# One half of an output projection multiplied inside the softmax branch that precedes it

## The reference

```python
ret = retention(...).reshape(B, S, RET_WIDTH) * silu(rg)        # 512 features
att = nsa(...).reshape(B, S, NSA_WIDTH) * silu(ng)              # 512 features
mixed = concatenate([ret, att], axis=-1)                        # 1024
y = rmsnorm(mixed @ w_out[l], g_post[l])                        # projection 2
x = x + gate * y
# second block
f = swiglu(rms_norm(h, g_ffn1_pre), w_ffn1_gate, w_ffn1_up, w_ffn1_down)
h = h + 0.5 * rms_norm(f, g_ffn1_post)
```

## Time and the profile before

| | us |
|---|---|
| three runs, median (lowest to highest) | 1502.58 (1501.13 to 1503.46) |
| span of the profiled execution | 1500.5 |
| TensorE busy | 1452.3 (97%) |
| VectorE busy | 828.7 (55%) |
| ScalarE busy | 683.7 (46%) |
| GpSimd busy | 201.9 (13%) |
| DMA engines, share of the span | 27.2% for the queue that loads the weights |

### The profile page before, as it was taken

The page is one execution under the profiler, slowest core; times in us unless marked ns, Lnnn a source line. Parts: engine busy times, 40 slices in busy tenths (PEclk is TensorE's granted clock), DMA queues, the critical chain, the costliest instruction groups (busy, mean ns, idle before and its releaser), DMA issues.

```text
span 1500.5 us, 22048 instructions
## 1 busy us (share of the span) xinstructions
PE 1452.3 (97%) x8524; PEld 1226.9 (82%) x8524; DVE 828.7 (55%) x1455; ACT 683.7 (46%) x1302; POOL 201.9 (13%) x319
## 2 busy tenths in 40 slices
PE   7999999899999999999999999989999999999997
PEld 4887876678988888888998777769988888888996
DVE  6678646776645444432275577574754444422474
ACT  4565536676542222221363556676532232321563
POOL 0000000443310000000130222451300000000221
PEclk9999999999999999999999999999999999999999
DMA  9542440004033333333404211503133333332321
GB/s 365 197 167 85 124 157 10 1 2 169 2 99 98 98 98 98 94 95 94 152 3 167 71 57 43 169 16 99 33 109 98 94 92 96 103 105 92 120 85 56
DMA packets 42148, 146.71 MB, mean 98 GB/s; under 512 B 4673, under 2 KB 7121, under 8 KB 41682
## 3 DMA queue, kind: packets, MB, share of 16 engines
q1 hardware_dynamic: 37986, 128.99, 27.2%
q0 software_dynamic: 3072, 15.71, 2.8%
q10 hardware_dynamic: 1008, 0.89, 0.2%
HBM read 141.39 MB, written 4.19 MB: 97 GB/s over the span
## 4 chain that ended last, share of the span: by engine, by line
PE 84%; DVE 9%; ACT 3%; issue 2%; DMA 1%; POOL 0%; DVEq 0%; SPq 0%; ACTq 0%; POOLq 0%
PE B L285 22%; PE B L287 22%; PE B L286 22%; PE CROW_P L285 3%; PE CROW_P L287 3%; PE CROW_P L286 3%; PE B L1789 2%; PE B L2025 1%; DVE AL L1381 1%; DVE WADA L1143 1%; PE CROW_P L1868 1%; ACT T L622 1%; PE CROW_P L1768 1%; ACT AH L622 1%; DVE WL L1110 1%
## 5 line engine op out<-in xcount | busy, mean ns | idle before, releaser
L285 PE MATMUL B<-UH,WH 128*128 128x512 f32 (+1 forms) x1008 | 374.7, 372 | 4.6 <-DVE WL L1110 3.7
L287 PE MATMUL B<-UH,WL 128*128 128x512 f32 (+1 forms) x1008 | 372.3, 369 | 0.0
L286 PE MATMUL B<-UL,WH 128*128 128x512 f32 (+1 forms) x1008 | 372.3, 369 | 0.0
L622 ACT ACTIVATE WH<-RAW 128x1024 fp32r<-128x1024 f32 x174 | 182.6, 1052 | 120.0 <-DMA RAW<-in_stream 111.6
L285 PEld LDWEIGHTS B<-UH,WH 128*128 128x128 f32 x1008 | 190.4, 189 | 38.0 <-issue 5.0
L286 PEld LDWEIGHTS B<-UL,WH 128*128 128x128 f32 x1008 | 190.3, 189 | 32.0
L287 PEld LDWEIGHTS B<-UH,WL 128*128 128x128 f32 x1008 | 190.2, 189 | 32.0
L1110 DVE TENSOR_TENSOR WL<-RAW,WH 128x1024 fp32r<-128x1024 f32 x94 | 116.0, 1240 | 143.8 <-ACT WH L622 143.7
L1462 DVE TENSOR_TENSOR WL<-RAW,WH 128x1024 fp32r<-128x1024 f32 x80 | 98.0, 1226 | 76.7 <-ACT WH L622 73.9
L622 ACT ACTIVATE T<-B 128x256 f32<-128x256 f32 (+5 forms) x186 | 86.5, 465 | 109.9 <-PE B L287 63.3
L622 ACT ACTIVATE T<-T 128x512 f32<-128x512 f32 (+3 forms) x131 | 68.7, 525 | 130.8 <-DVE T L1466 119.2
(11 more groups left out here) (419 smaller groups left out, 3146.2 us busy)
## 6 DMA issues: line engine op xcount, KB each, us to landing
RAW<-in_stream SPq DMA_DIRECT2D x202, 512.0 KB, 3.7
WADA<-in_w_ada SPq DMA_DIRECT2D x8, 1024.0 KB, 16.7
RAW<-in_stream SPq DMA_DIRECT2D x16, 384.0 KB, 3.5
WADA<-in_w_ada SPq DMA_DIRECT2D x2, 2048.0 KB, 11.5
W<-in_w POOLq DMA_DIRECT2D x2, 2048.0 KB, 12.1
X<-in_x SPq DMA_DIRECT2D x2, 1024.0 KB, 11.0
DECAY<-in_decay POOLq DMA_DIRECT2D x1, 2048.0 KB, 9.6
X<-in_x POOLq DMA_DIRECT2D x2, 1024.0 KB, 8.2
```

The lines of the kernel that those rows point to most:

```text
L285: nc.tensor.matmul(out, lh, rh, start=start, stop=False, **kw)
L286: nc.tensor.matmul(out, lh, rl, start=False, stop=False, **kw)
L287: return nc.tensor.matmul(out, ll, rh, start=False, stop=stop, **kw)
L622: return nc.scalar.activation(out, in_, func, **kw)
```

## The change

Retention's half of projection 2 is taken out of it and made of 32 steps. A step is one contraction tile k of 0 to 3 of one chunk c of 0 to 7, in the full width of 512 tokens (`part_step`). One step runs in each of rounds 5 to 9 and 12 to 35 of the softmax branch, after the scores and ahead of the transposes; the last three follow the branch. The steps use bank B5 alone, so the scores' ring has three banks, and scores m wait for `exp` at 2m-1, the first unit of round m-1. ScalarE copies each full chunk out of B5 to SBUF (`part_out`, into PART, 512 columns), after the round's first exponential.

The weights of projection 2 are loaded as pairs of half chunks, retention's halves first, into other places, and they are split earlier: high parts ahead of rounds 4, 9, 14, 19, 27, 34, 35 and 37, low parts ahead of rounds 5, 10, 15, 20, 28, 35 and twice 37. The first step of a chunk waits for the low part. What follows the branch (`mix_out`) multiplies tiles 4 to 7 only; VectorE adds PSUM and PART into Y_H, and ScalarE squares Y_H. The MLP's first four chunks go tile by tile through all four (`first_up`), first t = 0 and then t = 1, and `n_stats(1)` stands after all of them.

```diff
-        KEPT_AT = {"p1": (64, 72, 80, 88), "p2": (16, 24, 64, 72, 80, 32, 40, 88), ...
+        KEPT_AT = {"p1": (64, 72, 80, 88), "p2": ("w0", 16, 24, "w0", 16, 24, 64, 72), ...
+        PART = [at(f"PART{m}", OFF_U + ((16 if m < 4 else 0) + 2 * (m % 4)) * KB, [P, SEQ]) for m in range(8)]
-        S_BANK, PT_BANK = [B[2], B[3], B[4], B[5]], [B[6], B[7]]
+        S_BANK, PT_BANK = {"nsa": [B[2], B[3], B[4]], "band": [B[2], B[3], B[4], B[5]]}, [B[6], B[7]]
+        PART_ROUNDS = [5, 6, 7, 8, 9] + list(range(12, 36))
+        PART_STEPS = [(c, k) for c in range(8) for k in range(4)]
+        PART_AT = {m: PART_STEPS[n] for n, m in enumerate(PART_ROUNDS)}
+        PART_LEFT = PART_STEPS[len(PART_ROUNDS):]
+        PART_ENDS = {m: c for m, (c, k) in PART_AT.items() if k == 3}
# SyncE
+                if D_P2 <= d < D_P2 + 8:
+                    half, pair = divmod(d - D_P2, 4)
+                    sp.dma_start(RAW[:, slot, :].rearrange("p (m c) -> p m c", m=2),
+                                 a["stream"][D_P2 + 2 * pair:D_P2 + 2 * pair + 2, :, 512 * half:512 * half + 512].rearrange("m p c -> p m c")
+                                 ).then_inc(raw_here[slot], 16)
# ScalarE
+            def part_out(c):
+                wait(act, E["part"], c + 1)
+                E["part_out"].mark(f(PART[c][:, :], B[5][:, :], ACT.Copy))
...
                             tag["exp"].mark(f(S[:, 0:L], src[:, 0:L], ACT.Exp, ...))
+                            if tag is NSA and s == 0 and m in PART_ENDS:
+                                part_out(PART_ENDS[m])
# VectorE
                 if m == 4:
                     gn_m(2)
+                if m == 5:
+                    gn_m(3)
+                    lo_of_weights(D_P2)
                 if m == 6:
                     gn_lo(2)
-                    gn_m(3)
-                if m == 9:
+                if m == 7:
                     gn_lo(3)
+                if m in (10, 15, 20, 28, 35):
+                    lo_of_weights(D_P2 + (10, 15, 20, 28, 35).index(m) + 1)
+                if m == 37:
+                    lo_of_weights(D_P2 + 6)
+                    lo_of_weights(D_P2 + 7)
...
+            def mix_out(gain, scale):
+                def whole(t, m):
...
+                    E["y_copy"].mark(tt(Y_H[:, m, h], B[uses["p2", 8 * t + m][0]][:, h], PART[m][:, h], ALU.add))
+                wait(dve, E["part_out"], 8)
+                for m in range(8):
+                    whole(0, m)
+                    if 3 <= m < 7:
+                        lo_of_weights(D_F1 + m - 3)
...
+                for n in range(KT + 2):
+                    if n < 6:
+                        whole(1, n + 2)
+                    next_u(0, n, Y_H, gain, scale)
# TensorE
+            def part_step(c, k):
+                if k == 0:
+                    pe.wait_ge(w_lo, D_P2 + c // 2 + 1)
+                    wait(pe, E["part_out"], c)
+                if c == 0:
+                    wait(pe, E["gn_lo"], k + 1)
+                hi, lo = out_weights(c, k)
+                ins = mm3(B[5][:, :], hi, lo, MRH[:, k, :], MRL[:, k, :], k == 0, k == 3)
+                if k == 3:
+                    E["part"].mark(ins)
...
-                        wait(pe, tag["max" if pair[0]["bias"] is not None else "exp"], 2 * m - 2)
+                        if tag is NSA:
+                            wait(pe, tag["exp"], 2 * m - 1)
...
+                    if tag is NSA and m in PART_AT:
+                        part_step(*PART_AT[m])
...
+            def first_up(phase, d0, t, done):
+                h = cols_of(t)
+                for k in range(KT):
+                    wait(pe, E["nu_lo"], 8 * t + k + 1)
+                    for j in range(4):
...
+                        ins = mm3(B[j][:, h], wtile(WH, d0 + j, k), wtile(WL, d0 + j, k), UH[:, k, h], UL[:, k, h], k == 0, k == KT - 1)
+                        if k == KT - 1 and done is mm:
+                            ins.then_inc(mm, 1)
+                    if k == 3 and done is None:
+                        y_stats(t + 1)
+                    if k == 3 and done is mm:
+                        n_stats(t - 1)
+                if done is mm:
+                    n_stats(t)
```

More of the change, by code:

```diff
@@ L1431, in project_out @@
                     next_u(t, n, Y_H, gain, scale)
-                    if t and n >= 6:
+                    if n >= 6:
                         lo_of_weights(up + n - 6)
@@ L1837, in transposes, with softmax_pairs @@
                 return ins
-            def softmax_pairs(units, tag, ahead, first):
+            def part_step(c, k):
[8 more added lines that the diff above has]
+                    E["part"].mark(ins)
+            def softmax_pairs(units, tag, ahead, first, banks):
                 N = len(units) // 2
@@ L1922, in _, with mix_chunk, mix_out @@
             wait(pe, E["ret_p"], 32)
-            softmax_pairs(NSA_UNITS, NSA, nsa_ahead, nsa_first)
+            softmax_pairs(NSA_UNITS, NSA, nsa_ahead, nsa_first, S_BANK["nsa"])
+            for c, k in PART_LEFT:
+                part_step(c, k)
+            def mix_chunk(m, t, tiles, done):
+                h = cols_of(t)
+                for k in tiles:
+                    if t == 0 and m == 0:
+                        wait(pe, at_lo, {4: 1, 6: 2, 5: 3, 7: 4}[k])
+                    hi, lo = out_weights(m, k)
+                    ins = mm3(B[uses["p2", 8 * t + m][0]][:, h], hi, lo, UH[:, k, h], UL[:, k, h], k == 4, k == 7)
+                if done is mm:
+                    ins.then_inc(mm, 1)
+                elif done is not None:
+                    done.mark(ins)
+            def mix_out():
+                for m in range(6):
+                    wait(pe, *((NSA["exp"], 64), (NSA["exp"], 62), (at_x, 7), (at_x, 8), (NSA["lo"], 64), (E["part_out"], 8))[m])
+                    pe.wait_ge(w_lo, D_P2 + 4 + m // 2 + 1)
+                    mix_chunk(m, 0, (4, 6), None)
+                for m in range(6):
+                    mix_chunk(m, 0, (5, 7), E["half"])
+                for m in range(6, 8):
+                    bank_of("p2", m)
+                    pe.wait_ge(w_lo, D_P2 + 4 + m // 2 + 1)
+                    mix_chunk(m, 0, (4, 6, 5, 7), E["half"])
+                for m in range(8):
+                    bank_of("p2", 8 + m)
+                    mix_chunk(m, 1, (4, 6, 5, 7), mm)
+                    if m == 1:
+                        y_stats(0)
             def project_out(phase, d0, t, uh, ul, bank_free, then, ready):
@@ L1946, in mlp_up @@
                                ready=u_ready(t) if j == 0 else None)
-                n_stats(t)
-                for j in range(4):
+                if not by_tile:
+                    n_stats(t)
+                for j in range(0 if by_tile else 4):
                     half_chunk(d0 + j, B[j], *u_in, t + 1, mm, ready=u_ready(t + 1) if j == 0 else None)
@@ L1988, in mlp_down @@
                     E["half"].mark(ins) if n < 8 else ins.then_inc(mm, 1)
[L1990 to L1996, removed]
+            mix_out()
+            mlp_up("f1", D_F1, 0, 0, True)
             mlp_down("d1", D_D1, 2, 0)
```

121 lines of the change are left out of this document (82 added, 39 removed).

## The result

The changed kernel takes 1522.2 us (median of four runs, 1521.1 to 1524.4) beside 1501.9 us for the kernel before: ratio 1.0136, 95% interval 1.0122 to 1.0151. It is slower, by 20 us where 12 were forecast, and it lies above the range. The profiled execution spans 1522.6 us, 22.1 more than the one of before.

What follows compares the result with a forecast made beforehand. TensorE, busy 97% of the span, was taken as the bound. Rounds, steps and removed matmuls +5.7, projection 2's start +0.2, its statistics +1.3, the MLP's start +4.9: +12.1 us on 1502.6, thus 1514.7 us; range 1507 to 1520.

Steps and rivals of the forecast that it cites:

- with it nothing more is late: MLP's first half: with adds at 0.42 us, VectorE makes tiles in time, 2 to 3 us in hand; no added wait.
- The matmul exchange: TensorE: 23.04 us leave projection 2, 32 steps of 0.68 us (21.8 us) come in; by themselves 1.3 us won.
- The ring, rounds 12 to 31: Scores wait for the previous round's first exponential: 0.90, 0.33 or 0.18 us by round form, 7.1 us in all.
- Its rival: The ring costs nothing: 7.1 us fall away in rounds 12 to 31, about 2 in early ones; 1505.6 us, 12%.
- The ring, rounds 0 to 3: First four softmax rounds, before any step: the forecast had no term for a ring wait here, 0 us.
- Rounds 4 to 11: Five steps, the first held in round 5 by its weights' low part; round 5 ends 3.4 us late, +5.8 in all.
- Projection 2: Its start waits for the last low parts, +0.2 us; its statistics wait for VectorE's last square, +1.3 us.
- The MLP's start: Ahead of the MLP's loop nothing covers logarithm, exponential, table load, high part and low part: +4.9 us.
- The rival of the late chain: Tile-by-tile chain late, adds at 0.96 us, sums after TensorE's arrival: 3 to 5 us more, 1518 to 1520, 18%.
- The clock: TensorE's granted clock was read as 1.00, the 2.4 GHz level, in each window; no term for a lower clock.

Runs made afterwards that it cites:

- experiment 2: The changed kernel with each step behind the round's transposes, no longer ahead of them: 1513.1 us, ratio 1.0071.
- Experiments 1 to 3: Kernel before with only the three-bank ring: 1.0039; changed kernel with steps behind the transposes: 1.0071; changed kernel with ScalarE's first exponential ahead of the high parts: 1.0112.
- Experiment 5: The changed kernel with the ring of four banks and its old wait kept for rounds 0 to 3: 1517.8 us, ratio 1.0102.
- experiment 8: The changed kernel with VectorE's last add of the two halves moved right behind the last but one: 1518.5 us, ratio 1.0107.
- experiment 7: The changed kernel with the MLP's fifth chunk split early and the second half of its first four chunks in two pairs: 1514.6 us, ratio 1.0082.
- experiment 4: The changed kernel with the first five steps in rounds 6 to 10 instead of 5 to 9: 1519.1 us, ratio 1.0111.

## Why the prediction was wrong

In short: the large terms held, and the sum failed where it put a term at nothing. Three steps failed: the ring was not walked through rounds 0 to 3 (+2.7 us), "with it nothing more is late" overlooked the bank that the last add empties (+1.6 us), and each new wait was priced at its length only, without the lower clock behind it (+1.7 us from the loop on). These 6.0 us are what separates the 12.1 forecast from the change's own 18.0 in the profile; what the other terms were off cancels to 0.1.

**The matmul exchange** was sized a little short. A step costs 0.73 us where no wait is beside it, for the forecast's 0.68 (exponential first: 2.74 - 2.01 = 0.73; the three steps behind the branch: 388.47 to 390.67, 2.20 us). The step's first matmul takes 0.32 us to the next start, the others 0.23 (experiment 2: 303.10, 303.42, 303.65). So 32 steps are 23.4 us, not 21.8, and the exchange by itself wins nothing where 1.3 us were forecast. The sums of the rounds hide it: they came within 0.4 us in rounds 12 to 35, so another part of them was too high by about as much.

**The ring, rounds 12 to 31,** is right in mechanism, place and size: rounds of 256, 128 and 512 columns take 3.66, 3.16 and 3.57 us, where the old round, the step and the wait made 3.59, 3.09 and 3.49. Experiments 1 to 3 show it from three sides. Its rival fell.

**The ring, rounds 0 to 3:** here the working failed. The forecast took the rounds of a form from round 12 on and left out the first four, which have scores and exponentials without a step. It also read the window from 253.7 to 292.3 us as rounds 4 to 10 and their lead-in; it holds rounds 0 to 11, and rounds 0 to 3 are its first 9.7 us. TensorE's waits there (1.2 and 1.4 us behind an exponential) are 2.7 us. Experiment 5 also shows why it mattered less than it looks: rounds 4 and 5 take back most of it.

**Rounds 4 to 11:** +4.9 for +5.8. Round 5 is 3.6 us longer than before, where the forecast had it end 3.4 late. The chain was right, but part of that agreement is luck: behind the 2.9 us wait the granted clock was 0.59 for 3.9 us, which the forecast did not have.

**Projection 2:** +1.7 for +1.3 at its statistics, the rest as forecast. The adds took 0.42 us even where GpSimd was busy all through them, with 0.96 for an operation that reads only SBUF:

```profile
409.41 0.74 POOL L532 TENSOR_TENSOR T<-T,T 128x256 f32<-128x256 f32 x1 [2.75 <-ACT T L640]
409.42 0.42 DVE L1480 TENSOR_TENSOR Y_H<-B,PART 128x256 f32<-128x256 f32 x1 [2.35 <-PE B L288]
415.31 0.96 DVE L1176 SCALAR_TENSOR_TENSOR UL<-X,VECS,UH 128x256 fp32r<-128x256 f32 x1
```

The last one stands beside GpSimd's work from 415.07 to 415.99; without it the same operation takes 0.47 us (413.36). By the Trainium skill (SBUF — State Buffer, section "Who interferes with whom") the add, with one SBUF operand, should keep its time; the trace agrees.

**The MLP's start:** the gap of 4.9 us came at 4.89, by the chain as written, table load included (444.68 + 1.28 us, the next activation at 445.97). "With it nothing more is late" was the step that failed here: VectorE's last add empties a bank that the first half needs, and it stood behind two tiles' operations, some at 0.96 us. That cost 1.6 us, which experiment 8 gives back. The rival of the late chain had the right place but not this cause, and 3 to 5 us for it: the adds kept 0.42 us, and TensorE did not wait for the second half's sums. The forecast also missed a second lock behind the gap, the load of the fifth chunk, which costs nothing until the first is removed.

**The clock** was left out of the sum altogether. The forecast read 1.00 in every window of before and priced each new wait at its length only. The wait of 4.9 us cost 1.7 us more behind it (experiment 7; 1.6 to 2.8 us in the eight profiles that have this wait), that of round 5 a stretch at 0.59 (experiment 4). **The 4.0 us ahead of round 0** are no step's fault.

## What to carry to other kernels

Price a new idle of TensorE as its length and the half-speed stretch that may follow, and list every new wait's neighbours that are already in line behind it: a gap often has a second lock. When a ring gets shorter, walk its first rounds as well as its steady ones, and put the inserted work where the engine waits, behind what the other engines need, not ahead of it. Where the exchange itself wins nothing, idle time that can be filled (9.3 us here, by the forecast's count) is the whole prize of moving work, so the order must give back nothing else.

## What was not expected of the hardware

TensorE's granted clock fell to about half behind idle that is short beside the span. In the changed kernel it was 0.59 for 3.9 us behind 2.9 us of waiting and 0.70 for 5.6 us behind 4.9 us; behind 1.1 us (experiment 7) it stayed at 1.00. Executions differ in it: the unchanged work at 206 to 212 us was granted 0.50 to 0.52 in three of the thirteen profiles, the changed kernel's among them, and 1.00 in the others, and the bank's wait of 1.9 us was followed by 0.52 in experiment 2 and by 1.00 in experiment 5, whose windows are these:

```profile
411.00:413.00 2.00, 0.33 (x3) 0.12 (x2) 2.00 (x5) 0.82 (x3) 0.97 (x2) 1.00 0.04 8
413.00:417.00 4.00, 3.96 (x33) 3.97 (x34) 4.00 (x8) 1.93 (x6) 2.50 (x3) 1.00 0.00 0
```

What decides it between such executions stays open. One such stretch moved a single profiled execution by 2.4 us, more than several of the edits; so distances here are counted from stage to stage.
